# A single-core hybrid decoder block: routing of the expert layer token tile by token tile inside attention, with a slot table in DRAM

## What is computed

```python
def hierarchical_moe(u, w_rg, b_rg, w_re, b_re, w_gate, w_up, w_down):
    g_prob = softmax(xt @ w_rg + b_rg)             # 4 groups
    g_p, g_idx = lax.top_k(g_prob, 1)
    e_logits = (xt @ w_re + b_re) of group g_idx   # 8 experts in it
    e_p, e_idx = lax.top_k(softmax(e_logits), 2)
    gates = g_p * e_p / sum(e_p)
    # tokens sorted by expert into blocks of 128 rows; a block has one expert
    hdn = silu(xb @ w_gate[e]) * (xb @ w_up[e]);  y = hdn @ w_down[e]      # 1024 -> 512 -> 1024
    out = sum over a token's two experts of gate * y
```

## Time and profile before

| | us |
|---|---|
| median of 3 runs (lowest, highest) | 1449.18 (1448.6, 1456.89) |
| the profiled execution, time | 1456.25 |
| its span, first to last instruction | 1454.5 |
| PE, DVE, ACT, POOL busy | 1297.9, 840.0, 701.9, 222.2 |

### The profile page before, as it was taken

The page is one execution under the profiler, slowest core; times in us unless marked ns, Lnnn a source line. Parts: engine busy times, 40 slices in busy tenths (PEclk is TensorE's granted clock), DMA queues, the critical chain, the costliest instruction groups (busy, mean ns, idle before and its releaser), DMA issues.

```text
span 1454.5 us, 18404 instructions
## 1 busy us (share of the span) xinstructions
PE 1297.9 (89%) x7034; PEld 1065.8 (73%) x7034; DVE 840.0 (58%) x852; ACT 701.9 (48%) x857; POOL 222.2 (15%) x213
## 2 busy tenths in 40 slices
PE   4999999999899999999961399999999999999960
PEld 3999988999856666766641378888888888888850
DVE  6322243133443443434327578888888888888845
ACT  7111140244433433333321067777777777777740
POOL 3000002000000000000004112222222323333310
PEclk9999999999958999999985599999999999999985
DMA  7310035120021111101146069999999999999748
GB/s 224 88 59 1 1 127 185 37 59 1 3 85 44 45 44 44 44 1 44 44 202 289 24 241 380 384 380 377 389 382 379 383 375 380 380 380 377 275 168 346
DMA packets 55989, 278.97 MB, mean 192 GB/s; under 512 B 8992, under 2 KB 27440, under 8 KB 43648
## 3 DMA queue, kind: packets, MB, share of 16 engines
q1 hardware_dynamic: 40208, 240.23, 43.9%
q0 software_dynamic: 14576, 33.81, 6.2%
q10 hardware_dynamic: 1152, 4.19, 0.7%
HBM read 262.47 MB, written 33.55 MB: 204 GB/s over the span
## 4 chain that ended last, share of the span: by engine, by line
PE 84%; DVE 6%; ACT 4%; issue 3%; DMA 2%; SPq 1%; DVEq 0%; POOLq 0%; POOL 0%; ACTq 0%
PE ps L803 9%; PE ps L805 9%; PE ps L804 9%; PE ps L1054 8%; PE ps L1056 8%; PE ps L1055 8%; PE ps L905 6%; PE ps L872 5%; PE ps L1075 4%; PE ps L1077 4%; PE ps L1076 4%; PE ps L888 3%; PE ps L1043 2%; DMA y<-expert_rows 2%; PE ps L1062 1%
## 5 line engine op out<-in xcount | busy, mean ns | idle before, releaser
L1054 PE MATMUL ps<-wh,xh 128*128 128x512 f32 x512 | 205.9, 402 | 4.8 <-DVE xl L1728 4.8
L1056 PE MATMUL ps<-wh,xl 128*128 128x512 f32 x512 | 201.5, 394 | 0.0
L1055 PE MATMUL ps<-wl,xh 128*128 128x512 f32 x512 | 200.7, 392 | 0.0
L1728 DVE TENSOR_TENSOR wl<-wd,wh 128x2048 fp32r<-128x2048 f32 x64 | 143.8, 2288 | 31.5 <-ACT wh L1307 31.5
L1728 DVE TENSOR_TENSOR wl<-wu,wh 128x2048 fp32r<-128x2048 f32 x62 | 139.4, 2289 | 30.2 <-ACT wh L1307 28.2
L1728 DVE TENSOR_TENSOR wl<-wg,wh 128x2048 fp32r<-128x2048 f32 x62 | 139.4, 2288 | 9.8 <-ACT wh L1307 6.9
L1307 ACT ACTIVATE wh<-wg 128x2048 fp32r<-128x2048 f32 x64 | 118.7, 1905 | 6.6 <-PE ps L1056 6.6
L905 PE MATMUL ps<-pT,v 128*64 128x128 f32 (+1 forms) x704 | 121.6, 302 | 0.0
L1307 ACT ACTIVATE wh<-wd 128x2048 fp32r<-128x2048 f32 x64 | 119.1, 1916 | 0.0
L1054 PEld LDWEIGHTS ps<-wh,xh 128*128 128x128 f32 x512 | 97.1, 190 | 29.5 <-DVE wl L1728 5.7
L1307 ACT ACTIVATE wh<-wu 128x2048 fp32r<-128x2048 f32 x64 | 118.5, 1902 | 0.0
(11 more groups left out here) (298 smaller groups left out, 2625.6 us busy)
## 6 DMA issues: line engine op xcount, KB each, us to landing
wg<-in_w_gate SPq DMA_DIRECT2D x32, 2048.0 KB, 10.4
wu<-in_w_up SPq DMA_DIRECT2D x32, 2048.0 KB
wd<-in_w_down SPq DMA_DIRECT2D x32, 2048.0 KB
y<-expert_rows SPq DMA_DIRECT2D x16, 512.0 KB, 12.5
xin<-in_x SPq DMA_DIRECT2D x8, 512.0 KB, 8.7
zx<-in_x POOLq DMA_DIRECT2D x4, 1024.0 KB, 6.7
conv_part_rows<-zx POOLq DMA_DIRECT2D x16, 256.0 KB, 3.0
raw_c<-in_w_in SPq DMA_DIRECT2D x4, 1024.0 KB, 5.4
```

The source lines that it names most:

```text
L1054: mm(o, xh[:, k, :], wh[:, slot, k, :], start=(k == 0), stop=False)
L1055: mm(o, xh[:, k, :], wl[:, slot, k, :], start=False, stop=False)
L1056: last = mm(o, xl[:, k, :], wh[:, slot, k, :], start=False, stop=(k == KT - 1))
L1728: return V.tensor_tensor(dst, src, high_part.bitcast(F32), ALU.subtract)
```

## The change

Routing is spread over the tiles. The router product L now takes the 128 tokens as the stationary operand and gives token rows directly, 40 columns wide (4 groups, 4 of padding, 32 experts). Behind it VectorE finds group and experts of this tile with `max` and `max_index`, makes the one-hots and adds them to the running sum, 13 small instructions, and one for the gates. A new ring job G, one tile later, counts the ranks of the tile on TensorE by two products; VectorE turns each rank and expert into a slot number, row x 256 + column, with column = expert for the first 128 tokens of an expert and further columns for more. Three VectorE instructions and two of ScalarE make the gates.

GpSimd scatters, with two indirect DMAs of 128 words per tile, the row numbers into a table of 128 x 256 words in DRAM, which was filled with an invalid number at the start. After the last tile it reads the table back into SBUF as `tab`, and its columns serve as index columns for gather and scatter alike. For this u2 is written to DRAM twice, rows 0 to 1023 and 1024 to 2047, so that one number fits both.

LT, RANK and TABLE go. A job CNT gives the counts per expert; from them VectorE makes the number of the last block and announces `route_ready`, then makes the low gate parts of the first expert (GpSimd did), then the experts and columns of the further blocks, `blocks_ready`. GpSimd makes only the low up parts of the first expert, after the first two gathers. SP loads the second expert after the last L. For later blocks GpSimd loads the column number into a register.

```diff
+WC = 8 + NE
+STEPS = T // P
+TABC = STEPS * NE
...
-EXTRA = {2: "N", 3: "M", 4: "W", 6: "U", 7: "L"}
+EXTRA = {1: "G", 2: "N", 3: "M", 4: "W", 6: "U", 7: "L"}
+LAG = {"G": 2, "N": 1, "M": 1, "W": 1, "U": 1, "L": 1}
+TAIL = [("N", NT - 1), ("G", NT - 2), ("M", NT - 1), ("W", NT - 1), ("U", NT - 1), ("L", NT - 1), ("G", NT - 1)]
...
-            if i and h in EXTRA:
-                jobs.append((EXTRA[h], i - 1))
-    jobs += [(k, NT - 1) for k in ("N", "M", "W", "U", "L")]
-    jobs += [("LT", 0), ("RANK", 0), ("TABLE", 0)]
+            if h in EXTRA and i >= LAG[EXTRA[h]]:
+                jobs.append((EXTRA[h], i - LAG[EXTRA[h]]))
+    jobs += TAIL
+    jobs.append(("CNT", 0))
...
-        dram_u2 = nc.dram_tensor("u2_rows", [T, D], F32).ap()
+        dram_u2 = nc.dram_tensor("u2_rows", [2 * T, D], F32).ap()
...
+        dram_slots = nc.dram_tensor("slot_table", [P * TABC, 1], I32).ap()
...
-            sp.wait_ge(rows_out, 16 * NT)
-            wait_made(sp, ("LT", 0))
+            wait_made(sp, ("L", NT - 1))
             load_expert(1, 1)
...
+            sp.wait_ge(blocks_ready, 1)
             last = sp.value_load(last_pair[0:1, 0:1], min_val=NE - 2, max_val=NE + MAX_OVER - 1)
...
+            pool.wait_ge(consts, 2)
+            slot_rows = dram_slots.rearrange("(p c) n -> p (c n)", p=P)
+            pool.dma_start(slot_rows, tab[:, :]).then_inc(slots_clear, 16)
...
+            def place(i):
+                pool.wait_ge(slot_ready, i + 1)
+                for k in range(2):
+                    nc.gpsimd.indirect_dma_start(
+                        out=dram_slots[:, :], in_=aux[:, k, i:i + 1], in_offset=None,
+                        out_offset=bass.IndirectOffsetOnAxis(ap=sloti[:, k, i:i + 1].bitcast(U32), axis=0),
+                        bounds_check=last_slot, oob_is_err=False).then_inc(slots_out, 16)
+            last_slot = pool.to_reg(P * TABC - 1)
             for i in range(NT):
+                if i:
+                    place(i - 1)
                 wait_used(pool, ("W", i))
                 pool.dma_start(dram_h1[P * i:P * (i + 1), :], h1b[:, :]).then_inc(h1_out, 16)
                 pool.wait_ge(u2_ready, i + 1)
-                pool.dma_start(dram_u2[P * i:P * (i + 1), :], u2[:, :]).then_inc(rows_out, 16)
+                for k in range(2):
+                    pool.dma_start(dram_u2[T * k + P * i:T * k + P * (i + 1), :], u2[:, :]).then_inc(rows_out, 16)
             nc.gpsimd.memset(xg[:], 0.0).then_inc(pool_step, 1)
...
-            wait_made(pool, ("LT", 0))
-            for m, slot in (("g", 0), ("u", 1)):
-                for n in range(2):
-                    pool.wait_ge(w_high[m], n + 1)
-                    nc.gpsimd.tensor_tensor(half(wl, slot, n), half(raw[m], 0, n), half(wh, slot, n).bitcast(F32),
-                                            ALU.subtract).then_inc(w_low[m], 1)
-            pool.wait_ge(rows_out, 16 * NT)
-            pool.wait_ge(route_ready, 1)
-            last_token, last_row = pool.to_reg(T - 1), pool.to_reg(2 * T - 1)
+            place(NT - 1)
+            pool.wait_ge(slots_out, 16 * 2 * NT)
+            pool.dma_start(tab[:, :], slot_rows).then_inc(table_in, 16)
+            pool.wait_ge(rows_out, 32 * NT)
+            pool.wait_ge(table_in, 16)
...
+                nc.gpsimd.tensor_copy(idxg[:, s:s + 1], tab[:, s:s + 1]).then_inc(idx_ready, 1)
...
+            wait_made(pool, ("L", NT - 1))
+            for n in range(2):
+                pool.wait_ge(w_high["u"], n + 1)
+                nc.gpsimd.tensor_tensor(half(wl, 1, n), half(raw["u"], 0, n), half(wh, 1, n).bitcast(F32),
+                                        ALU.subtract).then_inc(w_low["u"], 1)
+            pool.wait_ge(route_ready, 1)
+            pool.wait_ge(blocks_ready, 1)
             last = pool.value_load(last_pair[0:1, 0:1], min_val=NE - 2, max_val=NE + MAX_OVER - 1)
+            def column(b):
+                if isinstance(b, int) and b < NE:
+                    return tab[:, b:b + 1]
+                c = pool.value_load(bcol[0:1, bass.ds(b, 1)], min_val=0, max_val=TABC - 1)
+                return tab[:, bass.ds(c, 1)]
...
-                else:
+                elif kind == "L":
                     wait_used(pe, ("U", i))
                     for k in range(KT):
-                        last = three(ps[0:NG + NE, b0, 0:P], [w[:, k, :] for w in (wrh, wrl)],
-                                     [u[:, k, :] for u in (u2Th, u2Tl)], k)
+                        last = three(ps[:, b0, 0:WC], [u[:, k, :] for u in (u2Th, u2Tl)],
+                                     [w[:, k, :] for w in (wrh, wrl)], k)
+                else:
+                    pe.wait_ge(both_ready, i + 1)
+                    mm(ps[:, b0, 0:NE], tris[:, :], both[:, i, :], start=True, stop=False)
+                    last = mm(ps[:, b0, 0:NE], ones[:, :], prev[:, i, :], start=False, stop=True)
                 done(job, last)
...
-            for kind in ("N", "M", "W", "U", "L"):
-                extra(kind, NT - 1)
-            job = ("LT", 0)
+                if n < NH and heads[n][1] in EXTRA and heads[n][0] >= LAG[EXTRA[heads[n][1]]]:
+                    extra(EXTRA[heads[n][1]], heads[n][0] - LAG[EXTRA[heads[n][1]]])
+            for kind, i in TAIL:
+                extra(kind, i)
+            job = ("CNT", 0)
             start(job)
...
+            done(job, mm(ps[:, 3 * side(job), 0:NE], ones[:, :], prev[:, NT, :], start=True, stop=True))
...
+                elif kind == "GE":
+                    act.wait_ge(gate_ask, i + 1)
+                    A(gex[:, :], lgt[:, 0:NG], ACT.Exp, bias=ngm[:, 0:1], accum_out=gsum[:, :])
+                    A(gratio[:, :], top8[:, 1, 1:2], ACT.Exp, bias=ngm[:, 1:2]).then_inc(gate_exp, 1)
...
+                if i >= 2 and h == 0:
+                    extra("GE", i - 2)
...
-                else:
+                elif kind == "L":
                     job = ("L", i)
                     wait_made(dve, job)
-                    V.tensor_scalar(lT[0:NG + NE, P * i:P * (i + 1)], ps[0:NG + NE, 3 * side(job), 0:P],
-                                    br_c[:, :], None, ALU.add).then_inc(used[side(job)], 1)
+                    V.tensor_tensor(lgt[:, :], ps[:, 3 * side(job), 0:WC], br_b[:, :], ALU.add).then_inc(used[side(job)], 1)
+                    wait_used(dve, job)
+                    then(V.max(top8[:, 0, :], lgt[:, 0:8]))
+                    then(V.max_index(top8i[:, 0, :], top8[:, 0, :], lgt[:, 0:8]))
+                    then(V.tensor_copy(gsel[:, :], top8i[:, 0, 0:1]))
+                    then(V.tensor_scalar(rk2[:, 0, :], iotag[:, :], gsel[:, :], NEG, ALU.not_equal, ALU.mult))
+                    then(V.tensor_tensor(rk2[:, 1, :], lgt[:, WC - NE:], rk2[:, 0, :], ALU.add))
+                    then(V.max(top8[:, 1, :], rk2[:, 1, :]))
+                    then(V.max_index(top8i[:, 1, :], top8[:, 1, :], rk2[:, 1, :]))
+                    then(V.tensor_copy(expid[:, :, i], top8i[:, 1, 0:2]))
+                    for k in range(2):
+                        then(V.tensor_scalar(one[:, k, :], iota128[:, 0:NE], expid[:, k, i:i + 1], None, ALU.is_equal))
+                    then(V.tensor_tensor(both[:, i, :], one[:, 0, :], one[:, 1, :], ALU.add))
+                    V.tensor_tensor(prev[:, i + 1, :], prev[:, i, :], both[:, i, :], ALU.add).then_inc(both_ready, 1)
+                    V.tensor_scalar(ngm[:, :], top8[:, :, 0], -1.0, None, ALU.mult).then_inc(gate_ask, 1)
+                else:
+                    job = ("G", i)
+                    wait_made(dve, job)
+                    V.tensor_tensor(rk2[:, :, :], one[:, :, :],
+                                    ps[:, 3 * side(job), 0:NE].unsqueeze(1).broadcast_to([P, 2, NE]),
+                                    ALU.mult).then_inc(used[side(job)], 1)
+                    wait_used(dve, job)
+                    then(V.tensor_reduce(rank[:, :], rk2[:, :, :], AX.X, ALU.add))
+                    then(V.tensor_tensor(over7[:, :, :], bc(rank[:, :], [P, 2, 7]),
+                                         lim[:, :].unsqueeze(1).broadcast_to([P, 2, 7]), ALU.is_ge))
+                    then(V.tensor_reduce(jblk[:, :], over7[:, :, :], AX.X, ALU.add))
+                    then(V.scalar_tensor_tensor(rank[:, :], rank[:, :], float(TABC), expid[:, :, i], ALU.mult, ALU.add))
+                    V.scalar_tensor_tensor(sloti[:, :, i], jblk[:, :], float(NE - P * TABC), rank[:, :],
+                                           ALU.mult, ALU.add).then_inc(slot_ready, 1)
+                    dve.wait_ge(gate_exp, i + 1)
+                    then(V.scalar_tensor_tensor(gden[:, :], gratio[:, :], 1.0, gsum[:, :], ALU.add, ALU.mult))
+                    then(V.reciprocal(gates[:, 0, i:i + 1], gden[:, :]))
+                    V.tensor_tensor(gates[:, 1, i:i + 1], gates[:, 0, i:i + 1], gratio[:, :], ALU.mult)
...
+            extras = {1: ("O",), 2: ("G", "N"), 3: ("M",), 4: ("AL", "W"), 5: ("U2",), 6: ("U",), 7: ("L",)}
...
```

(42 more changed lines are left out.)

242 lines of the change are left out of this document (87 added, 155 removed).

## The result

The changed kernel is slower: 1488.47 us (1480.82 to 1498.41) against 1448.89 for the kernel before on the same chip, a ratio of 1.027 with a 95% interval of 1.020 to 1.034. The forecast was 1436, the range 1420 to 1452. The profiled execution took 1488.17 us. The two profiled executions lie 32 us apart (spans of 1454.5 and 1486.5 us), the medians 40, since the profiled one of the kernel before took 1456.25 us, 7 more than its median.

What follows compares the result with a forecast made beforehand. TensorE was taken to bound attention and the expert loop, with a 56.6 us gap from last router product to first tokens. Paying 14 us in attention and saving 27 in the gap gave -13: 1436 us, range 1420 to 1452.

Steps and rivals of the forecast that it cites:

- Attention pays 14: In attention, routing work placed between heads adds 13.7 us, say 14 (4 to 27), on TensorE and VectorE.
- rival 3: In attention, stalls from 455 to 500 us send TensorE's clock down, losing up to 40 us: 1476; chance 0.09.
- the sign that I had named: In attention, TensorE's granted clock from 455 to 500 us must stay at 1.00.
- L on TensorE, 7 tiles: In attention, the router product's new form costs 0.4 us on each of seven tiles, 2.8 (0 to 8.4).
- G, ring and VectorE's G: In attention, rank products cost 4.2 us, score products waiting on the two-buffer ring 2.1, VectorE's nine rank instructions 1.8.
- VectorE's L chain: In attention, 13 small instructions delay the next heads' maxima and a late eviction: 2.8 us (1 to 8).
- 27 us saved in the hole: Between last router product and first tokens, 56.6 us before: tokens at 797, 27 us saved (22 to 35).
- the four slow instructions: In the old routing before the first tokens, small VectorE instructions took 3.51 to 4.45 us, otherwise 0.19; some 14 us.
- Hidden at no cost: Around routing and loop: low gate parts, block columns, up parts, second u2 copy, register loads and startup cost nothing.
- Rival 1: Between attention and loop, weight loads do not slow small transfers, scatter 3.2 us: 21 saved, 1428; chance 0.25.
- Rival 2: In attention, VectorE's chains come late for every head after them: bill 27 us, 1449, no change; chance 0.15.
- Rival 4: At the first tokens, GpSimd's up parts hold up VectorE's low part of them by 4.5 us: 1441; chance 0.08.

Runs made afterwards that it cites:

- the rank job alone: Kernel before plus, for tiles 0 to 6, two 32-column products and nine small VectorE instructions on constants, result unused: 1452.09 us, ratio 1.001.
- the chain alone: Kernel before plus 13 small VectorE instructions on constants behind the router product of tiles 0 to 6, result unused: 1464.4 us, ratio 1.010.

## Why the prediction was wrong, by its own steps

**Attention pays 14.** Wrong, and this is the step that failed: 60.4. The sum priced every added instruction by duration and gave none of them a say in the clock. The clock was there as rival 3, with 0.09, and the sign and the place were right in it; the sign that I had named, 1.00 from 455 to 500 us, came out as 0.70. Its mechanism was not right: I had stalls in mind, and TensorE's idle time in attention went down, from 10.1 to 8.5 us, with 28.00 of 28 us busy at 0.51. I should have read the earlier trace rows again: from 400 to 436 us the clock is 0.52 with TensorE busy 34.21 of 36. That row says that small products with next to no stall can go with the lower level. I quoted it and then argued with stalls. The rival's price, 40, was also too low against the 58 measured, as I gave it one stage; there are six falls from 447 us on. What the runs show in its place: L with 128 weight columns and 40 streamed, placed three heads after W, brings most of this low time. Alone it makes attention 48 us longer; in its old form, with all else of the change, attention is 49 us shorter.

The terms of the 14 compare like this. The second and third are each from a run of its own; the first is worked out from the pace of L's rows, the last from the granted clock in the windows of attention.

| term | predicted | measured |
|---|---|---|
| L on TensorE, 7 tiles | 2.8 (0 to 8.4) | 8.4: 24 x (0.11 - 0.06) = 1.2 a tile |
| G, ring and VectorE's G | 8.1 | 1.0 (the rank job alone) |
| VectorE's L chain | 2.8 (1 to 8) | 7.0, of which 3 low clock (low time 18 against 12) |
| the granted clock | 0 | 58: (127 - 12) / 2 |

The parts add to 71 (the 3 counted once), not to 60.4. By length times clock the other terms together got only 3 us in the changed kernel. Part of the gap is idle time: with the chain alone TensorE idles 14.2 of 299 us, in the changed kernel 8.5 of 352, and none of it in the slow windows shown. The rest is open, and 0.01 of the clock is worth 3.5 us here. The first three together came near what I said by errors of opposite sign, which is luck. Their bounds were also added up wrongly: they give 3.4 to 29.2, not 4 to 27; 60.4 lies outside either. L sat at the upper bound: with 128 weight columns a product takes 0.11 whether it streams 40, 80 or 120 columns, and with 40 weight columns and 128 streamed it takes 0.06. In the tail L cost 2.5 more, where I took 1.2.

**27 us saved in the hole.** Right in sum, 26.4 from the last output to the tokens, and in part by luck, as a scatter 3.0 below my figure made up for a read-back 3.4 above it. Between the last L and the tokens the gap is 27.8 us against 56.6, and I had said 30. Inside it: slot numbers 5.6 us after L's reading, 6.8 predicted; scatter 8.23, between the bounds of 3.2 and 11.2 and below the 11.2 I took; read-back 6.26, above its upper bound of 5.4, where I took 2.9; gather 4.21 against 4.4. Max and max_index, which I had no row for, take 0.17 to 0.20, and 0.25 to 0.28 with the load of their values. In my reading of the hole before, the four slow instructions hold 15.8 us beyond 0.19 each, where I wrote 14; no term of the sum used it.

**Hidden at no cost.** Right for the block columns (done at 848.5, tokens at 858.2), the up parts, the second copy of the rows, GpSimd's register loads (the loop is 576 us) and the startup (attention begins at the same time). The low gate parts were hidden, but not free: beside them the issue of the second scatter took 2.95 us instead of 1.02.

**Rival 1**, transfers not slowed: false here, since the loads are beside them, and true where they are not. Even there the 3.2 that I called the least was too high. The Trainium skill, DMA: Bandwidth & Descriptors, section on the anatomy of a SWDGE DMA, has about 2.0 us fixed and then the bytes; the runs agree on quiet engines for scatter and read-back (2.19 and 2.34 us), less for the gather of 512 KB (4.36 us, where an estimate by the page gives 3.2), and not beside weight loads (8.23 and 6.26), about which the fixed price says nothing.

**Rival 2**, attention pays double: its chain costs 7.0 us in the profile of the run with it alone, more than my 2.8 and less than the 16 that a bill of 27 would need.

**Rival 4**, GpSimd holds up VectorE's low part of the tokens: false. It runs at 861.24 in 1.22 us in the middle of GpSimd's 9.00. The Trainium skill, GPSIMD Engine Reference, section Key points, says that instructions with two inputs in SBUF, or in a two-port mode, contend; this instruction has one in PSUM, and the trace agrees.

## What to carry to other kernels

Read the granted clock next to the busy share, and price a product put between others not only by its own length: here the new form of 24 products a tile costs 8.4 us by its own pace and 48 in all, most of it through the clock of the work around them. Of two operand orders try first the one that loads few weight columns and streams many; if that can't be, try it beside dense work, or with its columns streamed two or three times. And try small transfers of a critical chain ahead of the bulk loads, for the whole length of the chain: held back for a part of it the loads only moved the delay (1438.94 against 1437.38), moving arithmetic alone gave nothing (1440.16), and both together, with the loads behind the whole chain, gave 5.5 us.

## What the runs showed of the hardware that I had not expected

- TensorE's granted clock falls while TensorE is busy without a gap (28.00 of 28 us at 0.51, 39.00 of 39 at 0.52). At tile 0 it stood at 1.00 until 24 products with 128 weight columns and 40 streamed had passed. It came back within a product of 512 columns twice, and three times among the products of the heads.
- With L in its old form it also fell once, for some 20 us (465 to 487), when 13 small VectorE instructions stood between the heads.
- The same 24 products a tile cost 38 us less when their columns were streamed three times, and 36 less when they stood behind a dense product.
- A product's pace went by its weights: 0.11 us apart with 128 weight columns for 40, 80 and 120 streamed; 0.06 with 40 weight columns and 128 streamed.
- An indirect scatter of 128 words landed in 2.19 us on quiet DMA engines, in 4.11 with its issue held up to 2.94 us, in 6.63 beside weight loads, and in 8.11 to 8.23 with both. In attention of the changed kernel, where the engines are nearly idle, the same transfers land in 2.4 us (from issue to landing, least, median, most):

```profile
DMA to landing us min/median/max: 2.2/2.4/8.2
```

- A gather of 128 rows took 4.21 to 4.36 us in the kernels shown with no new load beside it, 6.50 and 12.07 where one began with it.
- The issue of an indirect DMA on GpSimd took 1.02 us, and 2.94 beside a VectorE subtraction with both inputs in SBUF.

Open remains why the falls' places differ a little from execution to execution of one kernel: with the same code in attention the last output was taken at 750.30, 752.98, 753.07 and 759.02 us.
